# Gate, up and down products of four feed-forwards with a 512-column operand

## The chip, the cores and the metric

The kernel runs on one core of one Trainium2 chip. The time is the device time of one execution in microseconds (us). The engines are TensorE (PE in the profile; PEld is its loading of weights), VectorE (DVE), ScalarE (ACT), GpSimd (POOL) and SyncE (SP), which issues the loads from device memory. Each engine works through its own instructions in order and waits on semaphores for the others.

## The reference, cut to what matters

Two blocks of a model for 256 tokens of 1024 features. The first has two layers, each with a feed-forward ahead of the mixer and one behind it, and these four are what is changed; the second block (even and odd mixers and two other feed-forwards) follows.

```python
def rms_norm(x, w):
    xf = x.astype(jnp.float32)
    y = xf * lax.rsqrt(jnp.mean(xf * xf, axis=-1, keepdims=True) + NORM_EPS)
    return (y * w.astype(jnp.float32)).astype(x.dtype)

def swiglu(x, w_gate, w_up, w_down):
    return (jax.nn.silu(x @ w_gate) * (x @ w_up)) @ w_down
...
    for l in range(DEPTH):
        h = rms_norm(x, ffn1_norm[l])
        x = x + 0.5 * swiglu(h, ffn1_w_gate[l], ffn1_w_up[l], ffn1_w_down[l])
...
        x = x + merged @ w_out[l]

        h = rms_norm(x, ffn2_norm[l])
        x = x + 0.5 * swiglu(h, ffn2_w_gate[l], ffn2_w_up[l], ffn2_w_down[l])
    return x
```

DEPTH is 2, D_MODEL 1024, D_FF 2816.

## The kernel before, in words

**Names of the stages.** The feed-forwards are a0, b0, a1 and b1 (a ahead of the mixer, b behind it, the digit is the layer). The order is a0, mixer m0, b0, a1, mixer m1, b1, and then the second block. In the profiled execution b0 begins at about 445 us, a1 at 639 us and b1 at 1066 us.

**Layout.** The activations stand with features on the partitions: X holds 8 chunks of 128 features, 256 tokens each. The products take fp32 numbers as a sum of two parts, a high part rounded to the matmul's format and a low part that holds the rest. `product` (L681) therefore makes three matmuls for each pair of a 128x128 weight tile and a chunk of 256 columns: high weights by high activations (L685), high by low (L686), low by high (L687). Each loads its weights anew.

**Units.** The weights come in units of 1 MB: 1024x256 of a matrix, that is 8 tiles deep and 2 halves wide. SP loads unit m into one of three raw places, ACT rounds it to the high part in two halves of 128x1024 (`hi`, L1670), DVE subtracts for the low part (`lo`, L2479), and PE uses it. There are three places for raw units and three for split ones (AHEAD). On ACT and DVE the split of the unit three further on stands at the step of each unit, so that it can only begin when PE has left its place. A feed-forward has 22 units of gates and ups in turn (11 blocks), each of 48 matmuls before, and 12 units of the third matrix (`x` from 0 to 11: four blocks of output columns, each with 8, 8 and 6 tiles in depth, so that every third is smaller).

**Modulation units.** At the steps that the table ADA names (b0 and a1 the same ones, a0 and b1 others) a raw unit of the second block's modulation weights is loaded as well. It isn't split: DVE multiplies and adds it (L2454, four operations of 128x1024 for a unit) and every fourth time folds the sums (L2464). PE then makes a few tiny matmuls (L799). These units take places in the raw ring, so that the split behind one has a shorter lead.

**A block of gates and ups before.** The activations enter the gates without the norm's factor per token (`weighted` scales X by the norm's weights only), and the factor `rstd` is applied afterwards. The two banks of a block (one for each half of 128 outputs) hold the gates in columns 0 to 255 and the ups in 256 to 511. DVE multiplies both by rstd (L2666, L2667), ACT takes silu (L1853), POOL multiplies gate and up (L3554), ACT rounds the result (L1858), POOL takes the rest (L3559); these high and low parts of the 22 hidden chunks are what the third matrix is multiplied with. In b0, a1 and b1 the order on ACT in a block is: split for the gate's step, split for the up's step, silu twice, rounding twice. On DVE: the same two splits, then four products. In a0 the second split stands behind.

**The third matrix before.** Each block of it has two banks, of which 256 columns are used; DVE adds half of them to X (L2680), and ACT and POOL begin on the sum of squares for the next norm (L1730, L3507), and round X for the next stage (L1738).

Seven PSUM banks go round in a ring; PE waits at taking one until it has been read.

## Time and profile before

| | us |
|---|---|
| median of 3 runs | 2417.89 |
| lowest and highest | 2416.68, 2421.29 |
| the profiled execution | 2426.14 |
| its span, first to last instruction | 2424.2 |
| mean granted clock of TensorE, share of full | 0.994 |

The profiled execution is 8 us above the median. The page gives for each engine its busy time and share of the span. A matmul's busy time contains its way through the array, so that the records of neighbouring matmuls overlap; how fast they follow each other is read from their starts. In a timeline a bracket at the end of a row tells how long the engine sat idle before it and for whom.

### The profile page before, as it was taken

What the parts mean: (1) busy time and instruction counts of PE and PEld (TensorE: products, weight loads), DVE (VectorE), ACT (ScalarE), POOL (GpSimd) and SP (SyncE); (2) the same over time, 40 slices, a digit from 0 to 9 for tenths busy, and PEclk for the clock granted to TensorE, in tenths of its full rate; (3) what the DMA queues carried; (4) which work ended last, traced back from release to release, by engine and by line L of the source; (5) the groups of instructions that cost most, each with busy time, mean ns of one, the idle gap of its engine ahead of it and who ended that gap; (6) DMA issues with size and microseconds to landing.
All of it is one profiled execution on the core that took longest, in us unless ns stands there. A gap on an engine that the chain in (4) does not pass through costs nothing.

```text
span 2424.2 us, 40267 instructions
## 1 busy us (share of the span) xinstructions
PE 2386.3 (98%) x17001; PEld 2189.1 (90%) x17001; DVE 1610.2 (66%) x2428; ACT 1192.7 (49%) x1977; POOL 331.6 (14%) x362
## 2 busy tenths in 40 slices
PE   8999999999999999999999999999999999999998
PEld 7999889999999998999997758878889888889998
DVE  5676676887777677678866865765653655466753
ACT  5445665544444567655554642421333444455643
POOL 1311002232132100035330001000001000001000
PEclk9999999999999999999999989999999999999999
DMA  7768634676676783466763211345542433334552
GB/s 238 228 224 221 201 109 135 219 237 208 217 241 224 208 224 121 123 200 223 244 200 108 55 46 53 122 166 182 189 158 87 150 104 105 120 117 146 179 195 96
DMA packets 374113, 401.54 MB, mean 166 GB/s; under 512 B 44708, under 2 KB 346048, under 8 KB 373677
## 3 DMA queue, kind: packets, MB, share of 16 engines
q1 hardware_dynamic: 371160, 391.19, 51.3%
q10 hardware_dynamic: 2772, 7.78, 1.0%
q8 instruction: 133, 2.18, 0.4%
q14 instruction: 48, 0.39, 0.0%
HBM read 397.87 MB, written 4.22 MB: 166 GB/s over the span
## 4 chain that ended last, share of the span: by engine, by line
PE 82%; DVE 11%; ACT 3%; issue 1%; POOL 1%; SPq 1%; DMA 0%; DVEq 0%; ACTq 0%; POOLq 0%
PE bank L685 25%; PE bank L687 24%; PE bank L686 24%; DVE rounded L2479 4%; PE bank L693 3%; DVE plain L2454 2%; ACT rounded L1670 2%; PE bank L698 1%; PE bank L1109 1%; PE bank L1139 1%; DVE plain L2464 0%; DVE plain L2712 0%; DVE plain L2752 0%; PE bank L1310 0%; ACT plain L2073 0%
## 5 line engine op out<-in xcount | busy, mean ns | idle before, releaser
L685 PE MATMUL bank<-rounded 128*128 128x256 f32 (+2 forms) x3480 | 1079.5, 310 | 7.5 <-DVE rounded L2479 2.9
L686 PE MATMUL bank<-rounded 128*128 128x256 f32 (+2 forms) x3480 | 1065.3, 306 | 0.0
L687 PE MATMUL bank<-rounded 128*128 128x256 f32 (+2 forms) x3480 | 1065.2, 306 | 0.0
L2479 DVE TENSOR_TENSOR rounded<-plain,rounded 128x1024 fp32r<-128x1024 f32 (+1 forms) x630 | 737.0, 1217 | 409.1 <-ACT rounded L1670 408.9
L1670 ACT ACTIVATE rounded<-plain 128x1024 fp32r<-128x1024 f32 (+1 forms) x630 | 616.4, 1032 | 359.1 <-PE bank L687 267.7
L685 PEld LDWEIGHTS bank<-rounded 128*128 128x128 f32 x3480 | 665.3, 191 | 53.5 <-issue 9.6
L687 PEld LDWEIGHTS bank<-rounded 128*128 128x128 f32 x3480 | 665.4, 191 | 29.0
L686 PEld LDWEIGHTS bank<-rounded 128*128 128x128 f32 x3480 | 665.7, 191 | 28.0
L685 PE MATMUL bank<-rounded,rounded 128*128 128x256 f32 (+2 forms) x1472 | 449.0, 305 | 5.7 <-DVE rounded L2479 2.3
L687 PE MATMUL bank<-rounded,rounded 128*128 128x256 f32 (+2 forms) x1472 | 445.4, 303 | 0.0
L686 PE MATMUL bank<-rounded,rounded 128*128 128x256 f32 (+2 forms) x1472 | 445.4, 303 | 0.0
L685 PEld LDWEIGHTS bank<-rounded,rounded 128*128 128x128 f32 x1472 | 281.2, 191 | 19.2 <-DVE rounded L2479 3.9
L686 PEld LDWEIGHTS bank<-rounded,rounded 128*128 128x128 f32 x1472 | 281.3, 191 | 10.6
L687 PEld LDWEIGHTS bank<-rounded,rounded 128*128 128x128 f32 x1472 | 281.2, 191 | 10.6
L2454 DVE SCALAR_TENSOR_TENSOR plain<-plain 128x1024 f32<-128x1024 f32 x140 | 196.1, 1446 | 0.8 <-DMA plain<-in_ada_w 0.3
L3554 POOL TENSOR_TENSOR plain<-plain 128x256 f32<-128x256 f32 x88 | 77.4, 896 | 362.3 <-ACT plain L1853 287.3
L1853 ACT ACTIVATE plain<-plain 128x256 f32<-128x256 f32 x88 | 36.8, 418 | 171.5 <-DVE plain L2666 171.5
L3505 POOL COPY plain<-plain 128x256 f32<-128x256 f32 (+1 forms) x11 | 5.7, 517 | 762.1 <-ACT plain L1730 555.7
L3507 POOL TENSOR_TENSOR plain<-plain 128x256 f32<-128x256 f32 (+1 forms) x64 | 61.8, 966 | 292.0 <-ACT plain L1730 284.0
L1730 ACT ACTIVATE plain<-plain 128x256 f32<-128x256 f32 (+1 forms) x84 | 36.9, 442 | 117.6 <-DVE plain L2560 73.0
L3559 POOL TENSOR_TENSOR rounded<-plain,rounded 128x256 fp32r<-128x256 f32 x88 | 92.2, 1069 | 0.0
L2560 DVE SCALAR_TENSOR_TENSOR plain<-bank,plain 128x256 f32<-128x256 f32 x56 | 25.1, 480 | 95.5 <-PE bank L687 95.5
(313 smaller groups left out, 1861.1 us busy)
## 6 DMA issues: line engine op xcount, KB each, us to landing
plain<-in_mlp_w SPq DMA_DIRECT2D x64, 1024.0 KB, 5.3
plain<-in_ada_w SPq DMA_DIRECT2D x48, 1024.0 KB, 5.5
plain<-in_ffn_w_gate SPq DMA_DIRECT2D x44, 1024.0 KB, 5.7
plain<-in_ffn_w_up SPq DMA_DIRECT2D x44, 1024.0 KB, 5.5
plain<-in_ffn_w_down SPq DMA_DIRECT2D x32, 1024.0 KB, 5.6
plain<-in_w_in SPq DMA_DIRECT2D x32, 1024.0 KB, 5.4
plain<-in_od_w_in SPq DMA_DIRECT2D x32, 1024.0 KB, 5.4
plain<-in_ffn_w_down SPq DMA_DIRECT2D x16, 768.0 KB, 6.3
```

The source lines that it names most:

```text
L685: pe.matmul(dst, a[0], b[0], start=first and i == 0, stop=False)
L686: pe.matmul(dst, a[0], b[1], start=False, stop=False)
L687: ins = pe.matmul(dst, a[1], b[0], start=False, stop=last and i == n - 1)
L693: ins = pe.matmul(dst, a, b, start=first and i == 0, stop=last and i == n - 1)
L1670: act.activation(top, raw, ACT.Copy, scale=1.0).then_inc(*done(("hi", m, half)))
L1730: act.activation(sq[c % 2][:, 0:hi_ - lo], X[:, c, lo:hi_], ACT.Square, bias=0.0, scale=1.0).then_inc(*done((s, "sq", c)))
L1853: act.activation(f.sg[:, c % 4, :], f.sg[:, c % 4, :], ACT.Silu, bias=0.0, scale=1.0).then_inc(*done((s, "silu", c)))
L2454: dve.scalar_tensor_tensor(acc, raw[:, i, :], M.cc[:, k, v:v + 1], acc, MUL, ADD).then_inc(*done(*keys))
L2479: dve.tensor_tensor(low, raw, top, SUB).then_inc(*done(("lo", m, half)))
L3507: pool.tensor_tensor(acc, acc, sq[c % 2], ADD).then_inc(*done((s, "acc", c)))
L3554: pool.tensor_tensor(f.sg[:, c % 4, :], f.sg[:, c % 4, :], f.up[c % 4], MUL).then_inc(*done((s, "gu", c)))
L3559: pool.tensor_tensor(f.lr[:, c, :], f.sg[:, c % 4, :], f.hf[:, c, :], SUB).then_inc(*done((s, "hid", c)))
```

## The change

For blocks 5 to 10 of the gates and ups (WIDE) and blocks 0 to 2 of the third matrix, the low part of an activation chunk stands directly behind its high part, and both go in as one operand of 512 columns: `wide` makes one matmul of 512 columns (high weights by high and low) and one of 256 (low weights by high, added to the second half of the bank). A bank then holds two partial results of 256 columns, which have to be added. 

For the gates and ups each of these products takes a bank of its own, so that a block uses four. ACT first copies the second half of the bank to SBUF ("rest"), and DVE adds the first half to it. The result must then already have the norm's factor: in blocks 0 to 3 of each feed-forward DVE makes the 8 normalised chunks (`whole`, two a block, behind the block's four products), ACT rounds them, and POOL takes the rest, into the second place of a new view HW of the activations. PE waits for all eight at block 5. In blocks 5 to 10 the order within a block is another one on ACT and DVE: copies or additions of the gate, split for the gate's step, then copies or additions of the up, split for the up's step; silu behind the first split and rounding behind the second.

For the third matrix DVE updates X twice for each output chunk in blocks 0 to 2, the second update waiting for the first.

The room for `whole` is taken from two of the four accumulators of the modulation's sums.

```diff
@@ -110,6 +110,7 @@
 AHEAD = 3
+WIDE = 5
 LOW = AHEAD * (2048 + 4096) + 8192
...
@@ -325,6 +329,8 @@
         self.HSr = self.split_words(HS, 8192).rearrange("p (a c n) -> p a c n", a=2, c=8)
+        self.HWf = self.seen(HS, 8192).rearrange("p (c q n) -> p c q n", c=8, q=2)
+        self.HWr = self.split_words(HS, 8192).rearrange("p (c q n) -> p c q n", c=8, q=2)
         self.top = self.PHASE + 22 * 512 + 1024
@@ -372,7 +378,11 @@
         self.top = self.PHASE
-        b.hf, b.hr, b.lr = (grid(a, c=22) for a in self.take_split(22 * 256))
+        o = self.top
+        b.hl = self.split_words(o, 2 * 22 * 256).rearrange("p (c n) -> p c n", c=22)
+        b.hr, b.lr = b.hl[:, :, 0:256], b.hl[:, :, 256:512]
+        b.hf = self.seen(o, 2 * 22 * 256).rearrange("p (c n) -> p c n", c=22)[:, :, 0:256]
+        self.take(2 * 22 * 256)
         b.sg = grid(self.take(4 * 256), c=4)
...
@@ -687,6 +698,14 @@
 
+    def wide(dst, pairs, first=True, last=True):
+
+        n = len(pairs)
+        for i, (a, b) in enumerate(pairs):
+            pe.matmul(dst[:, 0:512], a[0], b, start=first and i == 0, stop=False)
+            ins = pe.matmul(dst[:, 256:512], a[1], b[:, 0:256], start=False, stop=last and i == n - 1)
+        return ins
+
     def plain(dst, pairs, first=True, last=True):
@@ -823,6 +842,20 @@
         for blk in range(11):
+            if blk >= WIDE:
+                for kind, step in (("g", 2 * blk), ("u", 2 * blk + 1)):
+                    m = U[s, kind, blk]
+                    bs = [bank(s, kind, blk, j) for j in range(2)]
+                    ready(m)
+                    for k in range(8) if (blk, kind) == (WIDE, "g") else ():
+                        for x in new(at(s, "whole", k)):
+                            pe.wait_ge(*x)
+                    for j in range(2):
+                        keys = [("unit", m)] if j else []
+                        wide(bs[j], [(part(m, k, j * 128), M.HWr[:, k, 1, :]) for k in range(8)]).then_inc(
+                            *done((s, kind, blk, j), *keys))
+                    fill(s, step)
+                continue
             m = U[s, "g", blk]
...
@@ -860,8 +893,11 @@
                             pe.wait_ge(*y)
-                    ins = product(bs[j][:, 0:256], [(part(m, k - k0, j * 128), (f.hr[:, k, :], f.lr[:, k, :]))],
-                                  k == 0, k == 21)
+                    if blk < 3:
+                        ins = wide(bs[j], [(part(m, k - k0, j * 128), f.hl[:, k, :])], k == 0, k == 21)
+                    else:
+                        ins = product(bs[j][:, 0:256], [(part(m, k - k0, j * 128), (f.hr[:, k, :], f.lr[:, k, :]))],
+                                      k == 0, k == 21)
                 keys = [("unit", m)] if j else []
...
@@ -1840,6 +1876,26 @@
                 root(was, M.one.rstd)
+            if blk >= WIDE:
+                for kind, dst in (("g", lambda c: f.sg[:, c % 4, :]), ("u", lambda c: f.up[c % 4])):
+                    for j in range(2):
+                        c = 2 * blk + j
+                        for x in new(at(s, kind, blk, j), at(s, "hid", c - 4)):
+                            act.wait_ge(*x)
+                        act.activation(dst(c), M.bank(s, kind, blk, j)[:, 256:512], ACT.Copy, scale=1.0).then_inc(
+                            *done((s, kind, "rest", c)))
+                    hi(U[s, kind, blk] + 3)
+                    fill(s, 2 * blk + (kind == "u"))
+                    for j in range(2):
+                        c = 2 * blk + j
+                        for x in new(at(s, "g", c) if kind == "g" else at(s, "gu", c)):
+                            act.wait_ge(*x)
+                        if kind == "g":
+                            act.activation(f.sg[:, c % 4, :], f.sg[:, c % 4, :], ACT.Silu, bias=0.0, scale=1.0).then_inc(
+                                *done((s, "silu", c)))
+                        else:
+                            act.activation(f.hr[:, c, :], f.sg[:, c % 4, :], ACT.Copy, scale=1.0).then_inc(*done((s, "hidhi", c)))
+                continue
             hi(U[s, "g", blk] + 3)
@@ -1856,6 +1912,10 @@
                 act.activation(f.hr[:, c, :], f.sg[:, c % 4, :], ACT.Copy, scale=1.0).then_inc(*done((s, "hidhi", c)))
+            for k in (2 * blk, 2 * blk + 1) if blk < 4 else ():
+                for x in new(at(s, "wholef", k)):
+                    act.wait_ge(*x)
+                act.activation(M.HWr[:, k, 1, 0:256], f.whole[:, k, :], ACT.Copy, scale=1.0).then_inc(*done((s, "wholehi", k)))
             if not early_next:
...
@@ -2652,6 +2713,17 @@
                 root(was, r)
+            if blk >= WIDE:
+                for kind, dst in (("g", lambda c: f.sg[:, c % 4, :]), ("u", lambda c: f.up[c % 4])):
+                    for j in range(2):
+                        c = 2 * blk + j
+                        for x in new(at(s, kind, "rest", c)):
+                            dve.wait_ge(*x)
+                        dve.tensor_tensor(dst(c), M.bank(s, kind, blk, j)[:, 0:256], dst(c), ADD).then_inc(
+                            *done((s, kind, c), ("free", s, kind, blk, j)))
+                    lo(U[s, kind, blk] + 3)
+                    fill(s, 2 * blk + (kind == "u"))
+                continue
             lo(U[s, "g", blk] + 3)
@@ -2665,6 +2737,9 @@
                 dve.tensor_tensor(f.up[c % 4], b[:, 256:512], r, MUL).then_inc(*done((s, "u", c), ("free", s, "gu", blk, j)))
+            for k in (2 * blk, 2 * blk + 1) if blk < 4 else ():
+                dve.scalar_tensor_tensor(f.whole[:, k, :], X[:, k, 0:256], col(f"{name}_norm", l * 8 + k), r, MUL, MUL).then_inc(
+                    *done((s, "wholef", k)))
             if not early_next:
@@ -2677,6 +2752,11 @@
                         dve.wait_ge(*y)
+                    if blk < 3:
+                        dve.scalar_tensor_tensor(X[:, o, 0:256], M.bank(s, "d", o)[:, 256:512], 0.5, X[:, o, 0:256], MUL,
+                                                 ADD).then_inc(*done())
+                        for y in new(L.last()):
+                            dve.wait_ge(*y)
                     dve.scalar_tensor_tensor(X[:, o, 0:256], M.bank(s, "d", o)[:, 0:256], 0.5, X[:, o, 0:256], MUL,
@@ -3557,6 +3637,11 @@
                 pool.tensor_tensor(f.lr[:, c, :], f.sg[:, c % 4, :], f.hf[:, c, :], SUB).then_inc(*done((s, "hid", c)))
+            for k in (2 * blk, 2 * blk + 1) if blk < 4 else ():
+                for x in new(at(s, "wholehi", k)):
+                    pool.wait_ge(*x)
+                pool.tensor_tensor(M.HWr[:, k, 1, 256:512], f.whole[:, k, :], M.HWf[:, k, 1, 0:256], SUB).then_inc(
+                    *done((s, "whole", k)))
             if s == "b1" and 7 <= 2 * blk + 1 < 14:
```

The pieces left out replace `hx(k, 0, 256)` by `M.hw(k)` in the narrow blocks (the same chunks in the new view), do the same in `weighted` on ACT and DVE, and set the places of `whole` and of the accumulators.

The order on ACT in b0, from silu of block 3 on: L1853 and L1858 are silu and rounding, L1670 the split's high part. Before:

```order
L1853 ACTIVATE plain1<-plain1 128x256 x2
L1858 ACTIVATE rounded1_50<-plain1 128x256 x2
L1670 ACTIVATE rounded0_49<-plain0 128x1024 x4
L1853 ACTIVATE plain1<-plain1 128x256 x2
L1858 ACTIVATE rounded1_50<-plain1 128x256 x2
L1670 ACTIVATE rounded0_49<-plain0 128x1024 x6
```

Now (L1909 silu, L1914 rounding, L1918 rounding of `whole`, L1706 the split, L1885 copy out of a bank, L1894 silu of a wide block):

```order
L1909 ACTIVATE plain1<-plain1 128x256 x2
L1914 ACTIVATE rounded1_50<-plain1 128x256 x2
L1918 ACTIVATE rounded0_49<-plain1 128x256 x2
L1706 ACTIVATE rounded0_49<-plain0 128x1024 x4
L1909 ACTIVATE plain1<-plain1 128x256 x2
L1914 ACTIVATE rounded1_50<-plain1 128x256 x2
L1885 ACTIVATE plain1<-bank3 128x256
L1885 ACTIVATE plain1<-bank4 128x256
L1706 ACTIVATE rounded0_49<-plain0 128x1024 x2
L1894 ACTIVATE plain1<-plain1 128x256 x2
```

Two roundings stand ahead of block 5's split, and two copies out of the gate's banks ahead of the split for block 6.

The order on DVE in b0, from the splits ahead of block 2's products on (L2666 and L2667 are the products by rstd, L2454 the modulation's sum, L2479 the split's low part). Before:

```order
L2479 TENSOR_TENSOR rounded0_49<-plain0,rounded0_49 128x1024 x6
L2666 TENSOR_TENSOR plain1<-bank6,plain1 128x256
L2667 TENSOR_TENSOR plain1<-bank6,plain1 128x256
L2666 TENSOR_TENSOR plain1<-bank0,plain1 128x256
L2667 TENSOR_TENSOR plain1<-bank0,plain1 128x256
L2454 SCALAR_TENSOR_TENSOR plain1<-plain0,plain1 128x1024 x4
L2479 TENSOR_TENSOR rounded0_49<-plain0,rounded0_49 128x1024 x2
```

Now (L2738 and L2739 the products by rstd, L2741 the whole products, L2514 the sum, L2539 the split):

```order
L2539 TENSOR_TENSOR rounded0_49<-plain0,rounded0_49 128x1024 x6
L2738 TENSOR_TENSOR plain1<-bank4,plain1 128x256
L2739 TENSOR_TENSOR plain1<-bank4,plain1 128x256
L2738 TENSOR_TENSOR plain1<-bank5,plain1 128x256
L2739 TENSOR_TENSOR plain1<-bank5,plain1 128x256
L2741 SCALAR_TENSOR_TENSOR plain1<-plain1 128x256 x2
L2514 SCALAR_TENSOR_TENSOR plain1<-plain0,plain1 128x1024 x4
L2539 TENSOR_TENSOR rounded0_49<-plain0,rounded0_49 128x1024 x2
```

Two whole products came between the block's products and the sum.

The order on DVE in b0's third matrix, from the sum with its folds (L2464) in unit 2 on; L2680 is the update of X, L2536 the low part of X's rounding. Before:

```order
L2454 SCALAR_TENSOR_TENSOR plain1<-plain0,plain1 128x1024 x4
L2464 TENSOR_REDUCE plain1<-plain1 128x32 x2
L2680 SCALAR_TENSOR_TENSOR plain1<-bank5,plain1 128x256
L2680 SCALAR_TENSOR_TENSOR plain1<-bank6,plain1 128x256
L2536 SCALAR_TENSOR_TENSOR rounded0_49<-plain1,rounded0_49 128x256
L2479 TENSOR_TENSOR rounded0_49<-plain0,rounded0_49 128x768 x2
```

Now (L2756 the update with a bank's second half, L2760 the one with its first):

```order
L2514 SCALAR_TENSOR_TENSOR plain1<-plain0,plain1 128x1024 x4
L2524 TENSOR_REDUCE plain1<-plain1 128x32 x2
L2756 SCALAR_TENSOR_TENSOR plain1<-bank1,plain1 128x256
L2760 SCALAR_TENSOR_TENSOR plain1<-bank1,plain1 128x256
L2756 SCALAR_TENSOR_TENSOR plain1<-bank2,plain1 128x256
L2760 SCALAR_TENSOR_TENSOR plain1<-bank2,plain1 128x256
L2596 SCALAR_TENSOR_TENSOR rounded0_49<-plain1,rounded0_49 128x256
L2539 TENSOR_TENSOR rounded0_49<-plain0,rounded0_49 128x768 x2
```

Each update of X has become two.

## Rows read from the trace of the kernel before

**Rows 1.** The page's busy times: busy us, share of the span, instructions.
```profile
PE 2386.3 (98%) x17001; PEld 2189.1 (90%) x17001; DVE 1610.2 (66%) x2428; ACT 1192.7 (49%) x1977; POOL 331.6 (14%) x362
```

**Rows 2.** Timeline of PE, 256 columns: start us, us, line, what; ten starts apart.
```profile
299.81 0.28 PE L685 MATMUL bank<-rounded 128*128 128x256 f32 x1
...
301.01 0.28 PE L686 MATMUL bank<-rounded 128*128 128x256 f32 x1
```

**Rows 3.** Timeline of PE, 512 columns, fifteen starts apart.
```profile
1639.93 0.39 PE L685 MATMUL bank<-rounded,rounded 128*128 128x512 f32 x1
...
1643.33 0.39 PE L685 MATMUL bank<-rounded,rounded 128*128 128x512 f32 x1
```

**Rows 4.** Stops of PE: timelines of b0 and a1, last the wait totals of a0.
```profile
515.65 0.38 PE L685 MATMUL bank<-rounded 128*128 128x256 f32 x1 [0.37 <-DVE rounded L2479]
...
579.78 0.19 PEld L685 LDWEIGHTS bank<-rounded,rounded 128*128 128x128 f32 x1 [0.35 <-DVE rounded L2479]
...
602.45 0.38 PE L685 MATMUL bank<-rounded,rounded 128*128 128x256 f32 x1 [0.64 <-DVE rounded L2479]
...
709.59 0.39 PE L685 MATMUL bank<-rounded 128*128 128x256 f32 x1 [0.37 <-DVE rounded L2479]
...
PEld bank L685 <- DVE rounded L2479: 1.0, 2, 0.7
```

**Rows 5.** Timeline of ACT in b0, blocks 2 to 6.
```profile
480.64 2.01 ACT L1670 ACTIVATE rounded<-plain 128x1024 fp32r<-128x1024 f32 x2 [1.64 <-PE bank L687]
...
496.75 3.88 ACT L1670 ACTIVATE rounded<-plain 128x1024 fp32r<-128x1024 f32 x4
...
511.83 0.42 ACT L1858 ACTIVATE rounded<-plain 128x256 fp32r<-128x256 f32 x1 [0.28 <-POOL plain L3554]
512.16 4.83 ACT L1670 ACTIVATE rounded<-plain 128x1024 fp32r<-128x1024 f32 x5
```

**Rows 6.** Timeline of DVE in the same stretch.
```profile
485.34 6.48 DVE L2454 SCALAR_TENSOR_TENSOR plain<-plain 128x1024 f32<-128x1024 f32 x4
491.75 2.35 DVE L2479 TENSOR_TENSOR rounded<-plain,rounded 128x1024 fp32r<-128x1024 f32 x2
...
497.83 4.63 DVE L2479 TENSOR_TENSOR rounded<-plain,rounded 128x1024 fp32r<-128x1024 f32 x4 [2.41 <-ACT rounded L1670]
502.38 4.87 DVE L2454 SCALAR_TENSOR_TENSOR plain<-plain 128x1024 f32<-128x1024 f32 x4
507.16 2.36 DVE L2464 TRANSPOSE_TENSOR_REDUCE plain<-plain 128x32 f32<-128x1024 f32 x2
...
513.24 3.50 DVE L2479 TENSOR_TENSOR rounded<-plain,rounded 128x1024 fp32r<-128x1024 f32 x3 [2.41 <-ACT rounded L1670]
```

**Rows 7.** The page's groups: busy us, mean ns of one, idle before.
```profile
L2560 DVE SCALAR_TENSOR_TENSOR plain<-bank,plain 128x256 f32<-128x256 f32 x56 | 25.1, 480 | 95.5 <-PE bank L687 95.5
```

**Rows 8.** Timeline of POOL in b0, blocks 2 and 3.
```profile
487.34 3.40 POOL L3559 TENSOR_TENSOR rounded<-plain,rounded 128x256 fp32r<-128x256 f32 x2
...
496.36 1.44 POOL L3559 TENSOR_TENSOR rounded<-plain,rounded 128x256 fp32r<-128x256 f32 x2
```

**Rows 9.** Timeline of ACT in a1, end of block 1.
```profile
674.58 2.01 ACT L1670 ACTIVATE rounded<-plain 128x1024 fp32r<-128x1024 f32 x2 [2.86 <-PE bank L687]
```

**Rows 10.** Timelines of DVE, POOL and PE in b1; the last is block 5's first matmul.
```profile
1119.43 6.48 DVE L2454 SCALAR_TENSOR_TENSOR plain<-plain 128x1024 f32<-128x1024 f32 x4
...
1121.43 3.40 POOL L3559 TENSOR_TENSOR rounded<-plain,rounded 128x256 fp32r<-128x256 f32 x2
...
1125.99 0.28 PE L685 MATMUL bank<-rounded 128*128 128x256 f32 x1
```

**Rows 11.** Timelines of DVE and ACT in b0's third matrix.
```profile
596.34 0.71 DVE L2680 SCALAR_TENSOR_TENSOR plain<-bank,plain 128x256 f32<-128x256 f32 x2
...
599.71 1.56 ACT L1670 ACTIVATE rounded<-plain 128x768 fp32r<-128x768 f32 x2
```

20 lines of the change are left out of this document (12 added, 8 removed).

## The prediction

> **What bounds the kernel now.** I read the page's busy times first [rows 1]: TensorE (PE) is busy for 2386 us of 2424, VectorE (DVE) two thirds, ScalarE (ACT) half, GpSimd (POOL) 14%. A busy PE is not a PE at its peak, so the next view is the timeline of PE in a stretch of matmuls with 256 columns: ten of them start in 1.20 us, one every 120 ns [rows 2]. In a stretch with 512 columns fifteen start in 3.40 us, one every 226.7 ns [rows 3]. Both streams load new weights for every matmul. The second column count costs 106.7 ns more than the first, so a matmul costs 106.7 ns per 256 columns (the 2.4 GHz level) and 13.3 ns for itself. The four feed-forwards run at this pace almost without a break; the third view, PE's stops, shows what ends the few: the low half of a weight block that DVE has just written (L2479), for 0.35 to 0.7 us each [rows 4]. So there are two things to weigh: the pace of PE, and how near the chain that splits the weights stands behind it.
>
> **What is saved.** Three matmuls of 256 columns (360 ns) become one of 512 and one of 256 (346.7 ns): 13.3 ns each time. One feed-forward has 6 blocks x 2 matrices x 2 halves x 8 chunks = 192 such groups in gates and ups, and 3 blocks x 2 halves x 22 chunks = 132 in the third matrix. 324 x 4 = 1296 groups, 1296 x 13.3 ns = 17.3 us. A mixed stream of both widths is not in the trace. Below, the saving is 0, if the 13.3 ns went with the columns; above I see nothing that would give more. I take 13.3, since each width alone shows it.
>
> The Trainium skill (TensorE: Matmul & The Clock Gate, "Wait — 56ns, not 53.3ns?") gives 2.5 ns as the fixed cost of a matmul at the fast clock. By it the saving would be 1296 x 2.5 ns = 3.2 us, an estimate; the rows say 13.3 for a matmul with its own weights, and the measurement decides.
>
> **What is added, and who stands behind it.** Per feed-forward: 8 products on DVE (two inputs in SBUF, 256 wide: the whole products), 8 copies on ACT, 8 subtractions on POOL, all in blocks 0 to 3; 24 copies out of PSUM on ACT in blocks 5 to 10; 6 more updates of X on DVE in the third matrix. Of the rest, the gates' additions on DVE take the place of as many products of the same size. By share none of this is much. But DVE, ACT and POOL run in order, and at one place the split of weights has no slack at all.
>
> *The chain up to block 6 (feed-forwards b0 and a1).* In b0 ACT last waited for PE at 480.64 us, idle for 1.64 us before it [rows 5]. From there to 515.6 us nothing on DVE and ACT waits for PE: split, products of block 2, four steps of the modulation's sum (485.34), split, products of block 3, POOL, ACT, split of block 5 (497.83), sum with two folds (502.38 to 509.5), products of block 4, ACT (512.16), split of block 6 (513.24 to 515.6) [rows 5, 6]. PE starts block 6 at 515.65, 0.37 us late [rows 4]. All that is put into this chain makes PE late in full. Its items:
> - Block 2's two whole products on DVE, ahead of the sum: 0.48 us is the longest that such an operation takes [rows 7], its step some 0.4: 0.8.
> - POOL's two subtractions of block 2 beside the sum and the split. The sum of four takes 4.87 us alone and 6.48 with three POOL operations and part of a fourth beside it [rows 6]: about 0.5 for each POOL operation, and POOL's pair goes from 1.44 to 3.40 [rows 8]. 2 x 0.5 = 1.0.
> - Block 3: two copies on ACT ahead of block 5's split, 2 x 0.33 (the step between ACT's 511.83 and 512.16 [rows 5]) = 0.65; POOL's product waits behind a whole product, 0.4; a whole subtraction beside the first split, 0.5.
> - Block 5: two copies out of PSUM stand ahead of the split of block 6 on ACT: 0.65.
> - Blocks 0 and 1 add the same, some 3.3 in all; in b0 ACT's wait of 1.64 swallows half, 1.6 is left; in a1 that wait is 2.86 [rows 9], 0.5 is left.
> Sum: 5.6 in b0, 4.5 in a1. The savings of block 5 (2 units x 16 x 13.3 ns = 0.43) are waited away too: 6.0 and 4.9. Below: without POOL's interference and with blocks 0 and 1 swallowed, 0.8 + 0.65 + 0.65 + 0.43 = 2.5 each. Above: the full blocks 0 and 1, and a late block 3 that also stops PE, 7.0 and 5.7.
>
> The rows of the sum show DVE and POOL slowing each other. Of this the Trainium skill (SBUF — State Buffer, "SBUF: two separate sides") says that a DVE operation with two SBUF inputs and a GpSimd operation lock each other out for a whole instruction. By that a subtraction would cost DVE its whole 0.72 us rather than 0.5, some 1 us more over both chains; the rows say less.
>
> *Feed-forward b1, block 5.* Its modulation units lie elsewhere; the sum of block 3 runs from 1119.43 [rows 10]. POOL ends its four operations at 1124.8 [rows 10], and the two whole subtractions come behind them at 1.7 us each, beside the sum: 1128.2, and 0.4 more for the shift of block 3's products. PE reaches block 5 at 1125.99 [rows 10] and needs all eight whole chunks there: 2.4. Below 0 (POOL alone, 0.7 each: 1126.3), above 3.5.
>
> *Third matrix, unit 5 (all four).* The sum with folds there ends with X's updates at 596.34; ACT squares, then splits from 599.71, and PE starts unit 5 at 602.45, 0.64 late [rows 4, 11]. The second update behind each first one makes this 0.45 later (one DVE operation, the other lies beside ACT), and PE comes 0.59 earlier for the saving of units 2 to 4, which is lost: 1.04 each in a0, b0, a1; b1 has a slack of 1.2, I take 0.2. Together 3.3; below 2.2, above 4.5.
>
> *Stops that go.* In blocks 5 to 10 the split stands ahead of ACT's silu chain. Block 10 to unit 1 of the third matrix (579.78, 0.35 [rows 4]) goes in b0 and a1; of a0's two stops [rows 4] the smaller, in block 9, goes for the same reason: 1.1 in all. Late next there is DVE with a sum before the additions, 0.5 to 1.8 us in hand by the same steps. Banks (seven, four of them now used in a block) come free 2.5 units before they are asked for, and two accumulators for four cost nothing, since DVE folds and sums in order itself.
>
> **The sum.** -17.3 + 6.0 + 4.9 + 2.4 + 3.3 - 1.1 = -1.8 us. The profiled execution took 2426.1 (span 2424.2 and 1.9 around it), so 2424.3 by its measure; it stood 8.2 above the median of 2417.9, and from that the forecast is 2416.1 us.
>
> **Rivals.**
> 1. The whole gain less little: POOL costs DVE nothing on the chain and the early blocks are swallowed. All lower ends: -17.3 + 2.5 + 2.5 + 0 + 2.2 - 1.1 = -11.2; with half of b1's wait -10: 2408. For it speaks that waits in front of PE's stops (1.64, 2.86) are there to swallow; against it the sum's 6.48 against 4.87.
> 2. Slower: the split of the wide blocks falls behind the unit it feeds. In blocks 5 to 10 DVE's additions must wait for PE and stand ahead of the split; with a sum (6.5 us beside POOL) between them, the split of the next unit ends 0.5 to 0.8 us ahead of PE by my steps, at two places in each feed-forward. It decides from a unit in which adding, sum and split pass the 11.1 us of two units; at 1 us for each of the eight places, and the chains at their upper ends (+1.8), the time is 2416.1 + 9.8 = 2426. Against it: half the units have no sum, and catch up.
> 3. The mixed stream saves nothing per matmul: then PE is also not early (2 x 0.43 + 3 x 0.59 less is lost): -1.8 + 17.3 - 2.6 = +13, 2431. Against it: both widths show the same 13.3.
>
> **Chances.** Forecast 0.55 (2410 to 2422), first rival 0.26, second 0.15, third 0.04. This kernel's measurement can tell 0.2% (4.8 us) from no change. Of the forecast's 0.55 some 0.03 lies beyond that on the fast side and 0.02 on the slow one; so faster 0.26 + 0.03 = 0.29, slower 0.15 + 0.04 + 0.02 = 0.21, same 0.50. The range goes from the first rival's 2408 to short of the second's: 2408 to 2425.
>
> **What the profile would show.** Right: pairs of wide and narrow matmuls every 347 ns; PE's stops in blocks 3 to 6 of b0 and a1 adding up to about 6.4 and 5.3 us against 0.4 before, ended by the split's low half; before block 5 of b1 for 2.4 us, ended by POOL; before unit 5 of the third matrix for 1.5 to 2 us; the stop at unit 1 gone. DVE's sum of block 2 longer than 6.5 us and POOL busy beside it. Wrong: stops before block 6 under 2 us (first rival), many stops inside blocks 7 to 10 (second), or a pair at 360 ns (third). It would also be wrong if a mixer or the stages behind changed their length, where nothing is edited.

## The result: 0.63% slower, and the profile after

The changed kernel takes 2436.42 us (median of four runs, 2428.53 to 2438.52) against 2418.61 us (four runs, 2416.68 to 2421.29). The ratio of their times is 1.0063, 95% interval 1.0052 to 1.0075: slower by some 15 us (the medians themselves are 17.8 us apart). The forecast was 2416.1, in a range of 2408 to 2425, so it was wrong in size and in sign. The profiled executions compare as 2436.45 (span 2434.6) to 2426.14 (span 2424.2), +10.3 us.

Against [rows 1] the page of the changed kernel reads (busy us, share of the span, instructions):

```profile
PE 2380.3 (98%) x15705; PEld 2122.7 (87%) x15705; DVE 1670.7 (69%) x2484; ACT 1228.0 (50%) x2105; POOL 389.1 (16%) x394
```

1296 matmuls are gone, as the change says. But PE's busy time fell by 6 us only, while PE's waits grew. Measured between the same units in both traces, the time moved like this:

| stretch | before | after | difference | forecast |
|---|---|---|---|---|
| start to the end of a0 | 215.0 | 212.3 | -2.7 | -3.7 |
| b0 | 194.0 | 200.8 | +6.8 | +2.4 |
| a1 | 191.5 | 195.6 | +4.0 | +1.3 |
| b1 | 191.9 | 195.9 | +4.0 | -1.7 |
| all else | | | -1.8 | 0 |

So 12.1 us were lost in the feed-forwards, where the forecast's terms say -1.8. Three views tell how.

**The stops.** PE's timeline (start, us, line, what, in brackets the idle time before it and what ended it); first b0, its blocks 3, 5 and 6 and unit 5 of the third matrix:

```profile
478.57 0.39 PE L696 MATMUL bank<-rounded 128*128 128x256 f32 x1 [0.96 <-DVE rounded L2539]
...
502.41 0.50 PE L705 MATMUL bank<-rounded 128*128 128x512 f32 x1 [0.54 <-DVE rounded L2539]
...
518.45 0.77 PE L705 MATMUL bank<-rounded 128*128 128x512 f32 x1 [4.28 <-DVE rounded L2539]
...
605.41 0.50 PE L705 MATMUL bank<-rounded,rounded 128*128 128x512 f32 x1 [1.76 <-DVE rounded L2539]
```

The same view, a1's blocks 5 and 6 and unit 5, then b1's block 5, block 7 (its up unit) and unit 5, ahead of them a0's unit 5:

```profile
173.10 0.50 PE L705 MATMUL bank<-rounded,rounded 128*128 128x512 f32 x1 [1.48 <-DVE rounded L2539]
...
702.25 0.50 PE L705 MATMUL bank<-rounded 128*128 128x512 f32 x1 [0.54 <-DVE rounded L2539]
...
718.28 0.47 PE L705 MATMUL bank<-rounded 128*128 128x512 f32 x1 [4.28 <-DVE rounded L2539]
...
805.45 0.50 PE L705 MATMUL bank<-rounded,rounded 128*128 128x512 f32 x1 [1.47 <-DVE rounded L2539]
...
1135.32 0.47 PE L705 MATMUL bank<-rounded 128*128 128x512 f32 x1 [1.19 <-POOL rounded L3643]
...
1166.01 0.79 PE L705 MATMUL bank<-rounded 128*128 128x512 f32 x1 [2.54 <-DVE rounded L2539]
...
1237.05 0.50 PE L705 MATMUL bank<-rounded,rounded 128*128 128x512 f32 x1 [1.24 <-DVE rounded L2539]
```

With 0.26 in a1's block 3 they add up to 20.54 us. The stops of before in the same stretches are 4.06: those of [rows 4], where a0's are 0.31 and 0.64 on PE, and two in a1:

```profile
773.72 0.19 PEld L685 LDWEIGHTS bank<-rounded,rounded 128*128 128x128 f32 x1 [0.35 <-DVE rounded L2479]
...
796.78 0.38 PE L685 MATMUL bank<-rounded,rounded 128*128 128x256 f32 x1 [1.03 <-DVE rounded L2479]
```

The growth is 16.5 us; the forecast has 15.5.

**The clock.** Windows of the changed kernel in b0; behind POOL's busy time stand PEclk, the DMA share and GB/s:

```profile
510.00:515.00 5.00, 4.16 (x31) 3.35 (x30) 3.27 (x7) 2.25 (x7) 2.47 (x4) 1.00 0.71 224
515.00:520.00 5.00, 1.55 (x5) 1.39 (x6) 4.52 (x7) 5.00 (x9) 1.56 (x3) 0.72 0.07 16
520.00:525.00 5.00, 5.00 (x20) 4.26 (x19) 5.00 (x4) 2.78 (x5) 3.59 (x3) 0.59 0.87 267
525.00:530.00 5.00, 5.00 (x30) 4.36 (x29) 3.44 (x7) 3.14 (x6) 0.00 (x0) 1.00 0.97 334
```

PE was idle for 4.28 us, and after that it works for some 6 us at the lower level (1.2 GHz): the windows count 20 matmuls between 520 and 525 and 30 in the next five microseconds. The same stands behind the 4.28 us stop of a1 (0.86 and 0.80), behind b1's 2.54 (0.66) and b0's 1.76 at unit 5 (0.66), not behind the shorter ones. Before, once a0 is under way, no stop of a feed-forward is longer than 1.03 us.

**The pace.** Two wide matmuls of the changed kernel, each time one unit (16 pairs) apart, in b0 and in a0:

```profile
549.23 0.39 PE L705 MATMUL bank<-rounded 128*128 128x512 f32 x1
...
554.77 0.39 PE L705 MATMUL bank<-rounded 128*128 128x512 f32 x1
```

```profile
121.83 0.40 PE L705 MATMUL bank<-rounded 128*128 128x512 f32 x1
...
127.47 0.40 PE L705 MATMUL bank<-rounded 128*128 128x512 f32 x1
```

5.54 us for 16 pairs is, within the rows' rounding, the 346.7 ns that [rows 2, 3] promised; 5.64 is 353. Both stretches are at the full clock and without a stop. Of all pairs at the full clock the mean is 351.05 ns, so the change saves 1296 x 8.95 = 11.6 us and not 17.3. The account of the feed-forwards: -11.6 + 16.5 = +4.9, and the other 7.2 us of the 12.1 are left for the low clock; the pairs that start in the four slow stretches named take, counted one by one in the trace, 7.3 us more than at the full clock.

### The profile page after: what moved, and what is told of

The parts are those of the page before. It is cut to its first block, busy times and chain, and to the rows that moved or that the text cites. A ratio compares the mean times of both kernels' runs of the same rounds, so it can differ in the third digit from the quotient of the medians.

```text
span 2434.6 us, 37834 instructions
## 1 busy us (share of the span) xinstructions
PE 2380.3 (98%) x15705; PEld 2122.7 (87%) x15705; DVE 1670.7 (69%) x2484; ACT 1228.0 (50%) x2105; POOL 389.1 (16%) x394
## 4 chain that ended last, share of the span: by engine, by line
PE 74%; DVE 17%; ACT 5%; issue 2%; POOL 1%; DMA 1%; ACTq 0%; DVEq 0%; POOLq 0%
PE bank L696 18%; PE bank L698 17%; PE bank L697 17%; PE bank L705 9%; DVE rounded L2539 6%; PE bank L706 5%; DVE plain L2514 4%; PE bank L712 3%; ACT rounded L1706 2%; PE bank L717 1%; DVE plain L2524 1%; PE bank L1145 1%; POOL plain L3634 1%; PE bank L1175 1%; DVE plain L2792 0%
## 5 line engine op out<-in xcount | busy, mean ns | idle before, releaser
L2539 DVE TENSOR_TENSOR rounded<-plain,rounded 128x1024 fp32r<-128x1024 f32 (+1 forms) x630 | 763.4, 1258 | 337.0 <-ACT rounded L1706 336.0
L696 PE MATMUL bank<-rounded 128*128 128x256 f32 (+2 forms) x2712 | 861.5, 318 | 7.6 <-DVE rounded L2539 3.1
L697 PE MATMUL bank<-rounded 128*128 128x256 f32 (+2 forms) x2712 | 847.7, 313 | 0.0
L698 PE MATMUL bank<-rounded 128*128 128x256 f32 (+2 forms) x2712 | 847.7, 313 | 0.0
L1706 ACT ACTIVATE rounded<-plain 128x1024 fp32r<-128x1024 f32 (+1 forms) x630 | 617.2, 1033 | 328.0 <-PE bank L698 190.7
L696 PEld LDWEIGHTS bank<-rounded 128*128 128x128 f32 x2712 | 517.6, 191 | 53.3 <-issue 9.2
L698 PEld LDWEIGHTS bank<-rounded 128*128 128x128 f32 x2712 | 517.8, 191 | 28.8
L697 PEld LDWEIGHTS bank<-rounded 128*128 128x128 f32 x2712 | 518.2, 191 | 27.9
L696 PE MATMUL bank<-rounded,rounded 128*128 128x256 f32 (+2 forms) x944 | 298.3, 316 | 3.1 <-POOL rounded L3677 2.2
L697 PE MATMUL bank<-rounded,rounded 128*128 128x256 f32 (+2 forms) x944 | 296.0, 314 | 0.0
L698 PE MATMUL bank<-rounded,rounded 128*128 128x256 f32 (+2 forms) x944 | 296.0, 314 | 0.0
L705 PE MATMUL bank<-rounded 128*128 128x512 f32 x768 | 276.4, 404 | 13.4 <-DVE rounded L2539 12.2
L706 PE MATMUL bank<-rounded 128*128 128x256 f32 x768 | 217.6, 283 | 0.0
L705 PE MATMUL bank<-rounded,rounded 128*128 128x512 f32 x528 | 188.3, 400 | 6.0 <-DVE rounded L2539 6.0
L696 PEld LDWEIGHTS bank<-rounded,rounded 128*128 128x128 f32 x944 | 179.9, 191 | 16.0 <-POOL rounded L3677 3.0
L2514 DVE SCALAR_TENSOR_TENSOR plain<-plain 128x1024 f32<-128x1024 f32 x140 | 192.8, 1423 | 0.8 <-DMA plain<-in_ada_w 0.2
L705 PEld LDWEIGHTS bank<-rounded 128*128 128x128 f32 x768 | 146.9, 191 | 49.6 <-DVE rounded L2539 12.8
L697 PEld LDWEIGHTS bank<-rounded,rounded 128*128 128x128 f32 x944 | 179.9, 191 | 10.6
L698 PEld LDWEIGHTS bank<-rounded,rounded 128*128 128x128 f32 x944 | 179.9, 191 | 10.6
L706 PE MATMUL bank<-rounded,rounded 128*128 128x256 f32 x528 | 148.6, 281 | 0.0
L706 PEld LDWEIGHTS bank<-rounded 128*128 128x128 f32 x768 | 147.7, 192 | 0.0
```

The lines of the kernel that those rows point to most:

```text
L696: pe.matmul(dst, a[0], b[0], start=first and i == 0, stop=False)
L697: pe.matmul(dst, a[0], b[1], start=False, stop=False)
L698: ins = pe.matmul(dst, a[1], b[0], start=False, stop=last and i == n - 1)
L705: pe.matmul(dst[:, 0:512], a[0], b, start=first and i == 0, stop=False)
L706: ins = pe.matmul(dst[:, 256:512], a[1], b[:, 0:256], start=False, stop=last and i == n - 1)
L1706: act.activation(top, raw, ACT.Copy, scale=1.0).then_inc(*done(("hi", m, half)))
```

## Experiments

Times are compared with runs of the kernel before on the same chip, of which the medians lay between 2418.9 and 2421.5 us. The edits are made to the changed kernel unless another is named.

### The parts, one at a time

**Third matrix alone** (L696 to L698 serve gates and ups again; the loop that makes whole products is switched off in the same way on DVE, ACT and POOL):

```diff
-WIDE = 5
+WIDE = 11
-            for k in (2 * blk, 2 * blk + 1) if blk < 4 else ():
+            for k in (2 * blk, 2 * blk + 1) if False else ():
```

> Only the third matrix is changed: its blocks 0 to 2 take high and low as one operand of 512 columns; gates and ups stay as before, nothing is added in blocks 0 to 3. Saved by the pace of the pairs: 132 x 4 x 13.3 ns = 7.0 us. Theory A (my prediction's step, a later split at unit 5): 3.3 us of it are given back, 2415. Theory B (the stops before unit 5 as the changed kernel shows them, 1.64, 1.92, 1.63 and 1.40 us in place of 0.80, 0.80, 1.19 and 0.04, and 1 us at the low clock behind the one of b0): 4.8 us given back, 2416.5. If the whole change loses evenly, this one should lose some 5 us as well: 2423.

2423.03 us, ratio 1.0009 (0.9996 to 1.0022): no gain from 7.0 us by the forecast's pace, so both theories miss. In its trace PE stops 1.76 us ahead of unit 5 in b0, and its pairs take 350.7 ns on average. By that pace 4.9 us are saved, and the stops at unit 5 give back 3.0; why the rest of the gain doesn't show, these rows don't tell.

**Gates and ups alone** (the same edit in DVE's update of X):

```diff
-                    if blk < 3:
+                    if False:
                         ins = wide(bs[j], [(part(m, k - k0, j * 128), f.hl[:, k, :])], k == 0, k == 21)
```

> Only gates and ups are changed (wide from block 5, with the whole products in blocks 0 to 3); the third matrix is as before. Saved by pace: 192 x 4 x 13.3 ns = 10.2 us. Theory A (chains as predicted): -10.2 + 6.0 + 4.9 + 2.4 - 1.1 = +2.0, 2420.6. Theory B (the 4.4 us stops before block 6 also bring the low clock behind them, some 4 us in b0, 2 in a1, 3 in b1, and b1 stops at the end of the gates): all of the loss is here, 2434 to 2437, and the granted clock of the five us behind each stop is below 0.9.

2437.74 us, ratio 1.0065 (1.0040 to 1.0090). The loss of the whole change is here.

**The whole products alone** (and the third matrix narrow, as above; the operations of blocks 0 to 3 stay):

```diff
-WIDE = 5
+WIDE = 11
```

> All matmuls as before (three of 256 columns for each group), but blocks 0 to 3 still make the whole products and their high and low halves, which nothing reads. It prices the added work of DVE, ACT and POOL by itself. Theory A (the chain counts it in full at two places): stops before block 6 of b0 and a1 of 3.5 to 5 us each, low clock behind them, nothing saved: 2418.6 + 5.2 + 4.1 + clock 3 to 6 = 2431 to 2434. Theory B (the added work is mostly hidden, and the stops come from the wide blocks' own order, rest copies and additions ahead of the split): within 3 us of before.

2437.58 us, ratio 1.0069 (1.0049 to 1.0089). PE stops ahead of block 6 in b0, with the matmuls of before:

```profile
521.01 0.39 PE L696 MATMUL bank<-rounded 128*128 128x256 f32 x1 [3.45 <-DVE rounded L2539]
```

The 24 added operations in each feed-forward's blocks 0 to 3 cost 17 us by themselves, which is above what theory A has (12 to 15). Nothing of that is peculiar to wide matmuls. PE's stops in b0's blocks 3 to 6 are 1.02, 0.54 and 3.45 us, 5.0 of the change's 5.8.

**All wide, no whole products** (the loops that make them are off as in the third matrix alone, and the result lacks the norm's factor):

```diff
-                        wide(bs[j], [(part(m, k, j * 128), M.HWr[:, k, 1, :]) for k in range(8)])
+                        wide(bs[j], [(part(m, k, j * 128), M.HWr[:, k, 0, :]) for k in range(8)])
```

> Gates, ups and third matrix wide as in the change, but the whole products, their copies and subtractions are left out: the wide blocks multiply the vector without the normalizing factor, so the output differs; the matmuls are the same in number and shape. Theory A: -17.3 + 1.3 (rest copies at two places) + 4.8 (unit 5) + 2 (end of the gates in b1), 2409 to 2411. Theory B: the stops before block 6 stay above 3 us, and the time is above 2425.

2417.91 us, ratio 0.9987 (0.9975 to 1.0000). The mirror image: without them the change is no slower than before, but it stays 7 us short of what theory A has. The pace is a part of that: its pairs take some 350 ns too. Ahead of block 6 PE still stops 1.21 us in b0 and a1, which is what the wide blocks' own order costs there.

### What a stop costs, and what GpSimd costs

**Stops filled with useless matmuls**:

```diff
+    def spare(dst, n):
+        for i in range(n):
+            pe.matmul(dst[:, 0:512], M.HWr[:, 0, 1, 0:128], M.HWr[:, 0, 1, :], start=True, stop=True)
...
+                    spare(bs[0], {("b0", "g", 6): 17, ("a1", "g", 6): 17, ("b1", "u", 7): 9}.get((s, kind, blk), 0))
                     ready(m)
```

> The changed kernel, with useless matmuls of 512 columns put on TensorE where it stops in the gates: 17 ahead of block 6 in b0 and a1 (3.9 us of the 4.4 us stop), 9 ahead of the up unit of block 7 in b1 (2.0 of 2.7 us); DVE, ACT and POOL do what they did. Theory A (the long stop lowers the granted clock, and that costs time of its own): the stretches at the low level behind these stops go (some 2.8 us in b0, 1.7 in a1, 1.6 in b1, perhaps 1.4 more behind b0's unit 5), granted clock above 0.95 there, 2429 to 2431. Theory B (the low clock is not tied to the stop's idleness, or other engines are late by as much anyway): the time stays at 2436 or grows by what the fillers delay.

2428.43 us, ratio 1.0035 (1.0021 to 1.0049): 7 us less with 43 matmuls more. The clock in the windows that were at 0.72 and 0.59:

```profile
515.00:520.00 5.00, 4.87 (x29) 3.57 (x28) 3.41 (x6) 4.73 (x11) 1.77 (x3) 1.00 0.09 30
520.00:525.00 5.00, 5.00 (x29) 4.34 (x29) 4.97 (x5) 4.09 (x7) 3.84 (x4) 1.00 0.75 220
```

This settles the clock's part: the same wait, spent at work, brings no low level, in b0, a1 (1.00 and 1.00) or b1 (1.00 and 1.00).

**GpSimd's subtractions cut to 8 columns** (in b0, a1 and b1; the low half is then not right):

```diff
-                pool.tensor_tensor(M.HWr[:, k, 1, 256:512], f.whole[:, k, :], M.HWf[:, k, 1, 0:256], SUB)
+                n = 256 if s == "a0" else 8
+                pool.tensor_tensor(M.HWr[:, k, 1, 256:256 + n], f.whole[:, k, 0:n], M.HWf[:, k, 1, 0:n], SUB)
```

> The changed kernel, but in b0, a1 and b1 GpSimd's subtractions for the whole products work on 8 columns in place of 256 (the low half is then not right, and the output differs): it prices the part that GpSimd takes in the chain before block 6. Theory A (my 0.5 us on DVE for each GpSimd operation beside it, three or four of them on the chain): the stops of blocks 3 to 6 of b0 shrink from 6.3 to about 4.5 us, a1's from 5.1 to 3.5, b1's wait for GpSimd (1.35) goes; with less low clock 2436.4 - 4.7 - 2 = 2429. Theory B (GpSimd costs DVE nothing; the work on DVE and ACT makes the chain): the stops before block 6 stay within 0.5 us, only b1's goes: 2435.

2425.38 us, ratio 1.0018 (1.0005 to 1.0031): 11 us gone, more than theory A has. PE's stops in the feed-forwards add up to 14.0 us in its trace, where the change has 20.5; the stops ahead of block 6 are 3.29 us in b0 and 2.81 in a1. DVE's whole products and sum of block 2 in the changed kernel and its sum in this one (each the kernel's timeline; 6.48 in [rows 6]):

```profile
484.31 1.52 DVE L2741 SCALAR_TENSOR_TENSOR plain<-plain 128x256 f32<-128x256 f32 x2
485.75 6.80 DVE L2514 SCALAR_TENSOR_TENSOR plain<-plain 128x1024 f32<-128x1024 f32 x4
```

```profile
485.19 5.83 DVE L2514 SCALAR_TENSOR_TENSOR plain<-plain 128x1024 f32<-128x1024 f32 x4
```

and two pairs of GpSimd's small subtractions, the first beside this sum, the second while DVE is idle:

```profile
487.51 2.38 POOL L3644 TENSOR_TENSOR rounded<-plain,rounded 128x8 fp32r<-128x8 f32 x2
...
497.32 0.37 POOL L3644 TENSOR_TENSOR rounded<-plain,rounded 128x8 fp32r<-128x8 f32 x2
```

An operation on 8 columns takes 1.19 us beside the sum and 0.19 us alone. The Trainium skill (SBUF — State Buffer, "SBUF: two separate sides") says that a DVE operation with two SBUF inputs, as the sum's are, and a GpSimd operation lock each other out for whole instructions; these rows agree. I had read the rule as a price on DVE, one operation long. In these rows the wait is on both sides: a GpSimd operation that could hardly be smaller waits for most of one of DVE's, and the two of 256 columns make DVE's sum 0.97 us longer, some 0.5 each, as I had taken.

### Moving what stands in the chain

**Later modulation units**:

```diff
-ADA = {"b0": [1, 4, 8, 11, 15, 18, 22, 26], "a1": [1, 4, 8, 11, 15, 18, 22, 26],
+ADA = {"b0": [1, 4, 9, 13, 16, 19, 22, 26], "a1": [1, 4, 9, 13, 16, 19, 22, 26],
```

> The changed kernel with b0's and a1's modulation units at steps 1, 4, 9, 13, 16, 19, 22, 26 in place of 1, 4, 8, 11, 15, 18, 22, 26: the sum with two folds (7.2 us of DVE) goes from ahead of block 6's split to behind it, and the sum of step 8 one unit later. Theory A (it is the pile of added work and this sum before one split): the 4.4 us stops before block 6 go, with the low clock behind them; at most 1 to 2 us come back where the sums stand now, among the wide blocks: 2436.4 - 8.8 - 4.5 + 3 = 2426. Theory B (DVE has no slack anywhere between blocks 3 and 8): the stop only moves to block 7, of 3 us or more, 2433 to 2436.

2425.63 us, ratio 1.0017 (1.0004 to 1.0030), as theory A has it. In b0 the 4.28 us stop becomes one of 0.88 us where the sum now stands:

```profile
529.20 0.50 PE L705 MATMUL bank<-rounded 128*128 128x512 f32 x1 [0.88 <-DVE rounded L2539]
```

**One whole product in each of blocks 0 to 7**, gates and ups wide from block 8 (WIDE is 8; the loop is the same on DVE, ACT and POOL):

```diff
-            for k in (2 * blk, 2 * blk + 1) if blk < 4 else ():
+            for k in (blk,) if blk < 8 else ():
```

> The changed kernel with one whole product in each of blocks 0 to 7 in place of two in blocks 0 to 3, and gates and ups wide from block 8 on. Saved by pace: gates 3 x 32 x 4 x 13.3 ns = 5.1 us, third matrix 7.0 us. Theory A (the chain up to block 6 counts every operation put in): it holds six whole products in place of eight and no rest copies; stops before block 6 of 2.5 to 3 us, hardly any low clock: 2418.6 - 12.1 + 5 + 4.8 + 1 = 2417 to 2420. Theory B (what matters is the two of block 2 and 3 alone): stop before block 6 under 2 us, 2413 to 2416.

2468.04 us, ratio 1.0197 (1.0180 to 1.0215). Both theories fail. In b1:

```profile
1205.55 0.76 PE L705 MATMUL bank<-rounded 128*128 128x512 f32 x1 [11.99 <-POOL rounded L3643]
```

Block 8 needs the whole product that block 7 makes behind its own results; the same wait is 8.19 us in b0 and a1 and 6.90 in a0. I had counted what the operations delay and not when their result is asked for.

**Third matrix wide in blocks 1 and 2 only**, the rest as in the third matrix alone:

```diff
-                    if blk < 3:
+                    if blk in (1, 2):
```

> Gates and ups as before; the third matrix is wide in blocks 1 and 2 only, so that block 0's two second updates of X don't stand in front of the split for unit 5. Groups: 88 x 4 = 352. Theory A (the traces so far: a pair takes 346.7 ns in some stretches and 353.3 in others, so 6.7 to 13.3 ns saved each; the stop at unit 5 back at 0.8 us): -2.3 to -4.7 and no loss, 2414 to 2416.5. Theory B (the later split at unit 5 is not from block 0's updates): the stop stays at 1.6 to 1.9 us and nothing is gained, 2418 to 2420.

2421.54 us, ratio 0.9995 (0.9984 to 1.0006). The stop at unit 5 is back at 0.84 us (1.76 with block 0 wide), so block 0's doubled updates made it longer. Theory A has the stop right and the time not: no gain is seen beyond the noise.

**Combined**: later modulation units in b0 and a1 as above and in b1, third matrix wide in blocks 1 and 2.

```diff
-       "b1": [2, 6, 10, 14, 17, 20, 23, 26],
+       "b1": [2, 6, 10, 15, 18, 20, 23, 26],
```

> The change with the modulation units of b0 and a1 at 1, 4, 9, 13, 16, 19, 22, 26, those of b1 at 2, 6, 10, 15, 18, 20, 23, 26 (14, 17 before), and the third matrix wide in blocks 1 and 2. Theory A (each stop has its own place and they add up): against the 2425.6 of the kernel with later modulation units, unit 5 gives back 3.3 us less 1.6 for the narrow block 0, and b1's 2.7 us stop in the up unit of block 7 shrinks to about 1, with its low clock: 2421. Theory B (DVE beside GpSimd is at its limit in b1): the stop in b1 moves a unit on and stays over 2 us: 2424.

2420.44 us, ratio 0.9996 (0.9985 to 1.0007). The remedies add up, to the time of before.

**The pair's order turned** for every second chunk:

```diff
+            if i % 2 == 0:
...
+            else:
+                pe.matmul(dst[:, 256:512], a[1], b[:, 0:256], start=False, stop=False)
+                ins = pe.matmul(dst[:, 0:512], a[0], b, start=False, stop=last and i == n - 1)
```

> The changed kernel, with the pair's order turned for every second chunk: wide, narrow, narrow, wide, and so on; nothing else changes. It asks why a pair takes 353.3 ns in most stretches and 346.7 in some. Theory A (the 6.7 ns hang on how a wide matmul's start stands to the end of the narrow one before it, so the order matters): the mean of two pairs changes clearly, to 693 ns or to more than 710. Theory B (they hang on something outside the pair, a phase that a stop sets): two pairs still take 693 in some stretches and 707 in others; the time stays within 3 us of 2436.

2430.95 us, ratio 1.0042 (1.0028 to 1.0057), 5 us less than the change. A unit half as in the rows on the pace (L706, L710 wide; L707, L709 narrow):

```profile
120.39 0.39 PE L706 MATMUL bank<-rounded 128*128 128x512 f32 x1
...
125.96 0.39 PE L706 MATMUL bank<-rounded 128*128 128x512 f32 x1
```

5.57 us for 16 pairs. The mean of two pairs is 696.9 ns, with 697 in nearly every stretch: neither the 707 nor the 693 of the fixed order. So the pace hangs on the order inside the stream (theory A), though not with the values that I named.

**The factor after the addition** in place of whole products (with the combined version's other edits; DVE waits for the addition first):

```diff
+                        dve.tensor_tensor(dst(c), dst(c), r, MUL).then_inc(*done((s, kind, c)))
```

> The combined version without whole products: the wide blocks multiply the vector as the narrow ones do, and DVE multiplies by the normalizing factor after the addition (24 more operations of 0.4 us on DVE in blocks 5 to 10 in place of 8 on DVE, 8 on ACT and 8 on GpSimd in blocks 0 to 3). Theory A (GpSimd beside DVE and the chain before block 6 were the cost): stops in blocks 3 to 6 under 1.5 us in all, no low clock, 2412 to 2415. Theory B (DVE is the limit in blocks 5 to 10 too, with its additions ahead of the split): new stops of 1 us and more at several wide units, 2420 to 2426.

2435.79 us, ratio 1.0061 (1.0046 to 1.0075), worse than theory B. Two stops of b0, in the wide blocks:

```profile
525.49 0.50 PE L705 MATMUL bank<-rounded 128*128 128x512 f32 x1 [2.26 <-DVE rounded L2539]
...
563.04 0.47 PE L705 MATMUL bank<-rounded 128*128 128x512 f32 x1 [2.08 <-DVE rounded L2539]
```

DVE has no room for 24 operations in blocks 5 to 10 either. This is the second rival's mechanism, with 24 operations where the change has none.

### Versions that beat both kernels

In all three, in a0, b0 and a1, the updates of X of the third matrix's block 0 stand one unit later on DVE, and ScalarE's squares with them:

```diff
-            if k0 == 16:
+            if x == 3 and s != "b1" or k0 == 16 and (x > 2 or s == "b1"):
                 for j in range(2):
-                    o = 2 * blk + j
+                    o = 2 * (blk if x > 3 else 0) + j
```

**The kernel before with this edit alone**:

> The kernel before, with one edit: in a0, b0 and a1 the updates of X for the third matrix's block 0, and ScalarE's rounding and squares behind them, stand behind the split of the fourth unit in place of ahead of it. Theory A (the stop ahead of unit 5 is the split that stands behind these updates): its 0.80, 0.80 and 1.19 us go: 2.8 us, some 0.1% less than before. Theory B (the sum of the modulation alone makes the split late, or the updates are then late for the next block's split): the stop stays or moves to unit 6, no change.

2418.44 us, ratio 0.9986 (0.9974 to 0.9997), only just clear of the noise. The three stops at unit 5 are gone from the trace.

**With the third matrix wide and turned, gates as before**:

> Gates and ups as before; the third matrix wide in blocks 0 to 2, with the pair's order turned for every second chunk, and block 0's updates behind the fourth unit's split as in the run beside it. 528 groups at 348.3 ns in place of 360: 6.2 us. Theory A (pace and stop are separate terms): 6.2 + 2.8 less 0.5 for b1, where the order of the updates stays: 0.35% less than before. Theory B (the doubled updates are late at the next place): about the 0.1% of third matrix wide in two blocks.

2411.95 us, ratio 0.9958 (0.9942 to 0.9975). The best version, faster than before by 0.42%, of which the edit alone is 0.14%.

**With gates and ups wide as well, and every remedy**:

> The whole change with every single remedy: later modulation units (b0, a1: 4, 9, 13, 16, 19 in place of 4, 8, 11, 15, 18; b1: 15, 18 in place of 14, 17), turned pairs in gates, ups and third matrix, block 0's updates behind the fourth unit's split. Theory A (the terms add): 1296 x 11.7 ns = 15.2 us of pace; stops left 3.5 us in b0, 2.3 in a1, 2.6 in b1 in place of 0.8, 0.8 and 0 (blocks), the ones at unit 5 gone (-2.8, +1 in b1), 2 us of low clock: -15.2 + 6.8 - 1.8 + 2 = -8, 0.35% less than before. Theory B (the whole products' load wins back what is saved): within 0.1% of before, and slower than the run with the third matrix alone.

2413.90 us, ratio 0.9973 (0.9961 to 0.9986). Also faster than both kernels, and, as far as these runs tell, not faster than the version with narrow gates (their intervals overlap): what gates and ups save at 348.5 ns a pair, 8.8 us, is at best what the whole products cost.

## Why the prediction was wrong

**What bounds the kernel**: right. PE's pace and the split behind DVE's chain decide, and the stops stood where the steps put them, but for b1's block 7.

**The chain up to block 6**: right in place and near in size. Forecast 6.0 and 4.9 (with the 0.4 of before, 6.4 and 5.3 to be seen); the rows show 0.96 + 0.54 + 4.28 = 5.8 in b0 and 5.1 in a1. That the whole products make most of it is shown by the run with the whole work alone (5.0 in b0); what the wide blocks' own order makes, by the run without whole products (1.21). That GpSimd has its part is shown by the run with 8 columns. Two whole products took 1.52 us on DVE, where I had 0.8 from [rows 7], whose operation reads one input from PSUM.

**b1, block 5**: 2.4 forecast (its steps as written add up to 2.6), 1.19 measured, ended by POOL as said. **Unit 5**: 3.3 forecast. The growth is 0.84, 1.12, 0.44 and, in b1, 1.24 where I had 0.2: 3.6 us.

**The second rival** came true at one place: in b1's block 7 the sum stands between additions and split, and PE stops for 2.54 us. DVE there (additions, sum, folds, additions, split):

```profile
1152.72 0.74 DVE L2722 TENSOR_TENSOR plain<-bank,plain 128x256 f32<-128x256 f32 x2
1153.39 6.35 DVE L2514 SCALAR_TENSOR_TENSOR plain<-plain 128x1024 f32<-128x1024 f32 x4
1159.66 2.36 DVE L2524 TRANSPOSE_TENSOR_REDUCE plain<-plain 128x32 f32<-128x1024 f32 x2
1161.95 0.71 DVE L2722 TENSOR_TENSOR plain<-bank,plain 128x256 f32<-128x256 f32 x2
1162.59 3.37 DVE L2539 TENSOR_TENSOR rounded<-plain,rounded 128x1024 fp32r<-128x1024 f32 x2
```

I had priced eight such places at 1 us and given them 0.15; one was enough to matter.

**Two steps of the sum failed.** The first is its first term, 13.3 ns a group. Each width alone does show it, and I took a stream of both to be the sum of two pure ones; it was 8.95 ns, 5.7 us less. My bounds had 0 below, so this alone would have left the forecast in its range. The second is a term that isn't in the sum: what comes behind a stop. I had forecast stops of some 4 us, in a kernel whose longest in these stretches was 1.03, and priced each at its own length. Behind the long ones the clock stays at its lower level: some 7 us more, given back by the run that keeps PE busy. With these two, -1.8 + 5.7 + 7.2 + 1.0 (stops) = +12.1, as in the table.

**The base** was the third error, and in microseconds the largest. I took 8.2 us off for what the profiled execution of before stood above its median, as if the changed kernel's profiled execution would stand as high above its own. It doesn't: it took 2436.45, and the median is 2436.42. So from 2416.1 to 2436.4 the account is 5.7 + 7.2 + 1.0 - 1.8 (all else, in the table) + 8.2 = 20.3 us. It also tells why the profiles are 10.3 us apart and the medians 17.8: before's profiled execution stands 7.5 above the median of 2418.61.

The traces show where before's profiled execution lost its time: between 1372 and 1450 us, behind the feed-forwards. Counted from the end, the last version here takes 8.2 us less there than the kernel before, the changed kernel 6.7 more than that version, the combined one 1.4 more. The clock goes with it. Windows of before, then of the last version:

```profile
1400.00:1420.00 20.00, 17.88 (x116) 13.11 (x117) 12.94 (x27) 13.02 (x28) 0.00 (x0) 0.88 0.21 62
1420.00:1440.00 20.00, 20.00 (x38) 8.11 (x37) 5.06 (x8) 5.87 (x8) 0.00 (x0) 0.78 0.13 44
1440.00:1460.00 20.00, 20.00 (x78) 14.81 (x77) 18.29 (x31) 7.50 (x13) 0.00 (x0) 0.83 0.01 2
```

```profile
1400.00:1420.00 20.00, 17.88 (x89) 9.97 (x88) 11.28 (x17) 11.56 (x19) 0.00 (x0) 1.00 0.16 52
1420.00:1440.00 20.00, 20.00 (x70) 12.44 (x69) 13.00 (x20) 9.64 (x15) 0.00 (x0) 0.87 0.00 1
1440.00:1460.00 20.00, 20.00 (x89) 17.06 (x88) 12.35 (x29) 3.12 (x8) 0.00 (x0) 0.96 0.00 0
```

The mean granted clock of an execution tells its time as well. Of the 85 executions of before beside these experiments, the 28 with 0.997 took 2416.1 to 2419.8 us, and the 16 with 0.993 or 0.994 took 2424.8 to 2427.8; the profiled one has 0.994. Of the changed kernel's four, three have 0.990 or 0.991, and the one with 0.995 is the fastest, 2428.53 us. Why executions of one kernel differ there is not shown.

## What to carry to other kernels

Where PE is the bound, price a new stop twice: by its length, and by the slow stretch that may come behind it once it is longer than those that the profile shows at the full clock. Compare a profiled execution with its own median, and with its granted clock, before a difference is carried over to another kernel. A change that buys a few nanoseconds per matmul with work on the engines that feed PE must be priced at the one place where these have no slack. Try its parts apart: here the cheap part, improved, was worth 0.4% (with 0.14% for a reordering that the kernel before can have too), and the dear part nothing. And a saving per matmul read from uniform streams should be measured in the mixed one.
